# Modulation chunks behind the first attention, expert loads from the state stage on, and expert weights in pieces of 8 KB

## The reference

```python
c_act = silu(c)
mod = c_act @ w_mod + b_mod                 # 6 x 1024 columns
sh1, sc1, gt1, sh2, sc2, gt2 = split(mod, 6)
h = layer_norm(x) * (1 + sc1) + sh1
y = hybrid_mixer(h, ...)                    # state-space mixer + attention, gated, then @ w_o
x = layer_norm(ALPHA * x + (1 + gt1) * y, ln1_g, ln1_b)
h = layer_norm(x) * (1 + sc2) + sh2
gates = top 2 of 16 experts per token       # softmax over 4 groups, 4 experts in each
out = sum_e gates[:, e] * ((silu(h @ w_gate[e]) * (h @ w_up[e])) @ w_down[e])
x = layer_norm(ALPHA * x + (1 + gt2) * out, ln2_g, ln2_b)
```

## Time and profile before

| | us |
|---|---|
| median of three runs | 1687.82 |
| span of the profiled execution | 1684.1 |
| first attention to the loop over experts | 200 to 355 |
| loop over the eight pairs of experts | 355.5 to 585.8 |
| second block | from 600 |
| TensorE busy | 1594.6 (95%) |
| VectorE busy | 936.2 (56%) |
| ScalarE busy | 655.0 (39%) |
| DMA, queue q1 (all loads of SP) | 326.94 MB, 54.2% of 16 engines |

### The profile page before, as it was taken

The page is one execution under the profiler, slowest core; times in us unless marked ns, Lnnn a source line. Parts: engine busy times, 40 slices in busy tenths (PEclk is TensorE's granted clock), DMA queues, the critical chain, the costliest instruction groups (busy, mean ns, idle before and its releaser), DMA issues.

```text
span 1684.1 us, 22446 instructions
## 1 busy us (share of the span) xinstructions
PE 1594.6 (95%) x9391; PEld 1239.9 (74%) x9391; DVE 936.2 (56%) x1380; ACT 655.0 (39%) x962; POOL 27.4 (2%) x89
## 2 busy tenths in 40 slices
PE   5999999989999879999999999999999999999998
PEld 1998655454445468687888899988768778889986
DVE  3876666632222266466675566545456567556653
ACT  2543420111111144565644534435355644544441
POOL 1000010100000000000000000000000000000000
PEclk9999999999999989999999999999999999999999
DMA  9555518999999924423354356545424235536651
GB/s 310 193 177 200 202 55 296 332 383 404 393 357 410 389 97 150 125 70 131 127 197 154 122 179 200 193 152 199 144 85 150 101 125 176 174 120 194 200 176 74
DMA packets 165376, 333.29 MB, mean 198 GB/s; under 512 B 17699, under 2 KB 69157, under 8 KB 165285
## 3 DMA queue, kind: packets, MB, share of 16 engines
q1 hardware_dynamic: 159728, 326.94, 54.2%
q10 hardware_dynamic: 5558, 5.06, 0.9%
HBM read 330.94 MB, written 1.05 MB: 197 GB/s over the span
## 4 chain that ended last, share of the span: by engine, by line
PE 77%; DVE 10%; DMA 7%; ACT 4%; issue 1%; POOL 0%; ACTq 0%; SPq 0%; POOLq 0%; DVEq 0%
PE ps_g L726 19%; PE ps_g L707 15%; PE ps_g L1262 5%; PE ps_g L1130 5%; DMA arena<-in_w_up_dram 4%; PE ps_s L1518 4%; PE ps_p L1518 3%; PE ps_o L774 3%; PE ps_g L867 3%; DVE ring_r L2266 2%; PE ps_p L707 2%; DMA ring<-in_w_mod_dram 1%; PE ps_x L680 1%; PE ps_g L1485 1%; PE ps_g L1406 1%
## 5 line engine op out<-in xcount | busy, mean ns | idle before, releaser
L2266 DVE TENSOR_TENSOR ring_r<-ring,late_w 128x4096 fp32r<-128x4096 f32 (+1 forms) x50 | 217.0, 4339 | 153.4 <-ACT late_w L1834 153.4
L1834 ACT ACTIVATE late_w<-ring 128x4096 fp32r<-128x4096 f32 (+1 forms) x50 | 178.1, 3563 | 126.8 <-PE ps_p L1518 42.8
L726 PE MATMUL ps_g<-hf_high,ring_r 128*128 128x256 f32 x640 | 178.9, 280 | 0.0
L726 PE MATMUL ps_g<-hf_high,late_w 128*128 128x256 f32 x576 | 162.1, 282 | 0.0
L726 PE MATMUL ps_g<-h_t_r,late_w 128*128 128x256 f32 x576 | 161.3, 280 | 0.0
L726 PEld LDWEIGHTS ps_g<-hf_high,ring_r 128*128 128x128 f32 x640 | 121.9, 190 | 0.0
L726 PEld LDWEIGHTS ps_g<-h_t_r,late_w 128*128 128x128 f32 x576 | 108.7, 189 | 0.0
L726 PEld LDWEIGHTS ps_g<-hf_high,late_w 128*128 128x128 f32 x576 | 108.1, 188 | 0.0
L1858 ACT ACTIVATE arena<-arena,neg_max 128x256 f32<-128x256 f32 (+1 forms) x160 | 71.5, 449 | 40.4 <-DVE neg_max L2321 40.4
L1130 PE MATMUL ps_g<-arena 128*64 128x512 f32 x288 | 85.9, 599 | 0.0
L707 PE MATMUL ps_g<-early_w,first_low 128*128 128x512 f32 (+1 forms) x176 | 68.7, 390 | 4.1 <-ACT arena L1820 2.2
(11 more groups left out here) (697 smaller groups left out, 3710.7 us busy)
## 6 DMA issues: line engine op xcount, KB each, us to landing
ring<-in_w_in_dram SPq DMA_DIRECT2D x31, 2048.0 KB, 7.9
ring<-in_w_gate_up_dram SPq DMA_DIRECT2D x44, 1024.0 KB, 7.4
arena<-in_w_down_dram SPq DMA_DIRECT2D x16, 2048.0 KB, 14.3
ring<-in_w_mod_dram SPq DMA_DIRECT2D x10, 2048.0 KB, 11.3
ring<-in_w_down_dram SPq DMA_DIRECT2D x10, 2048.0 KB, 7.9
arena<-in_w_up_dram SPq DMA_DIRECT2D x8, 2048.0 KB, 18.7
ring<-in_w_gate_dram SPq DMA_DIRECT2D x8, 2048.0 KB, 16.0
ring<-in_w_up_dram SPq DMA_DIRECT2D x4, 2048.0 KB, 19.1
```

The costliest lines, as they stand in the source:

```text
L726: ins = pe.matmul(b.ap[:, (f % 2) * SEQ:(f % 2 + 1) * SEQ], a[:, k, f * P:(f + 1) * P], x[:, k, :], start=k == 0 and i == 0, stop=k == nk ...
L1834: act.activation(high_of(name, rnd)[:, 0:n], ring[:, slot, 0:n], ACT.Copy).then_inc(high_ready.sem, 1)
L2266: dve.tensor_tensor(ring_r[:, slot, 0:n], ring[:, slot, 0:n], high_of(name, rnd)[:, 0:n].bitcast(F32), ALU.subtract).then_inc(low_ready.se ...
```

## The change

Chunks 10 and 11 of the modulation are loaded behind `att`, and VectorE adds them up ahead of its gating of the two halves of the attention product. Chunks 6 and 7 are loaded next, and TensorE takes their strips in the state stage, one behind the second `xs` transpose and the other in the middle of the `seg` products; `gs1`, `mod4` and `mod5` follow. The slots of the ring are now in a table. `down1` and `down0` of pair 0 and both gates of pair 1 are loaded during the state stage and the `so` products, `gate1`, `up1`, `up0` and `gate0` of pair 0 as slots come free. The gates of pair 1 have other places in the arena, and small tiles of the loop have moved for that. All expert chunks are cut in pieces of 8 KB: four rows of 512 or two rows of 1024 a piece. So the channels of `h2` stand in groups of four and not of two (`GROUPED`), which the copies of chunks 6 to 9, the norm `normed`, the router's weights and the hidden values of an expert follow.

```diff
-MOD_SUMMED = [8, 9, 4, 10, 11]
+MOD_SUMMED = [8, 9, 10, 11, 4]

 MOD_LATE = (10, 11)
 FIRST_CHUNKS = (MOD_FIRST + ["xbc0"] + [f"xbc{i}" for i in range(1, 4)] + ["q", "k", "v", "z0", "z1", "ga0", "ga1", "mod8", "gs0", "mod9", "att",
-                "gs1", "mod4", "mod5", "so0", "so1", "o0", "o1", "mod6", "mod7"])
+                "mod10", "mod11", "mod6", "mod7", "gs1", "mod4", "mod5", "so0", "so1", "o0", "o1"])
+
+FIRST_SLOTS = [j % 3 for j in range(FIRST_CHUNKS.index("mod6"))] + [1, 2, 0, 1, 2, 0, 1, 2, 0]
+assert len(FIRST_SLOTS) == len(FIRST_CHUNKS)
+LAYER_FIRST_SLOT = 1
...
-        odd_w = arena[:, 0:SLOT].rearrange("p (k n) -> p k n", n=HALF), [arena[:, lo:lo + SLOT // 2].rearrange("p (k n) -> p k n", n=HALF) for lo in (12 * D, GATES_AT - 2 * D)]
-        odd_up = x_rows, arena[:, 14 * D:16 * D].rearrange("p (t n) -> p t n", n=D)
+        odd_w = [arena[:, lo:lo + SLOT].rearrange("p (k n) -> p k n", n=HALF) for lo in (8 * D, 12 * D)]
+        odd_up = x_rows, arena[:, GATES_AT - 2 * D:GATES_AT].rearrange("p (t n) -> p t n", n=D)
...
+        def strips_bank(i):
+
+            return PT if i in (6, 7) else mod_bank(i)
+
+        def by_group(v):
+            return v.rearrange("p (k s q) -> p k q s", s=GROUPED, q=P)
+
+        def in_groups(v):
+            return v.rearrange("p (k q s) -> p k q s", s=GROUPED, q=P)
...
                 ins.then_inc(b.full, 1)
+                if r == 1:
+                    mod_strips(6)
             claim(S, "cb")
             for c in range(TB):
                 for g in range(SSD_GROUPS):
@@ -974,6 +990,8 @@
                                     conv[:, 12 + g, c * P:(c + 1) * P], start=True, stop=True)
             ins.then_inc(S.full, 1)
             for c in range(TB):
+                if c == 1:
+                    mod_strips(7)
                 for g in range(SSD_GROUPS):
...
             product_block("o1", 1, mg_turned)
-            mod_strips(6)
-            mod_strips(7)
             strips_sum(6)
...
-                w = w.rearrange("(k p) n -> p k n", p=P) if name.startswith("down") else w.rearrange("(k p s) n -> p k (s n)", p=P, s=2)
+                w = w.rearrange("(k p s) n -> p k (s n)", p=P, s=2 if name.startswith("down") else GROUPED)
                 sync.dma_start(keys(pair_w[j], w.shape[1], w.shape[2]), w).then_inc(expert_landed[j], 16)
+
+            def load_odd_gate(p, e):
+
+                w = t["w_gate"][0, 2 * p + e].rearrange("(k p s) n -> p k (s n)", p=P, s=GROUPED)
+                sync.dma_start(odd_w[e].rearrange("p (k s) n -> p k (s n)", s=GROUPED), w).then_inc(odd_landed[e], 16)
...
+                if name == "mod5":
+                    sync.wait_ge(G1.full, G1.nth("first", "att1"))
+                    load_expert("down1", 0)
                 if name == "o0":
                     sync.wait_ge(S.full, S.nth("first", "yo"))
                     sync.wait_ge(decay_ready, TB * SSD_GROUPS)
-                    for j, i in enumerate(MOD_LATE):
-                        sync.dma_start(keys(pair_w[4 + j], KD, HALF), sources("first", MOD_CHUNKS[i], 0)[0]).then_inc(late_landed[j], 16)
-                if name == "mod6":
+                    load_expert("down0", 0)
+                    sync.wait_ge(PT.full, PT.nth("first", "yd1"))
+                    load_odd_gate(1, 1)
+                    sync.wait_ge(O.full, O.nth("first", "gy11"))
+                    load_odd_gate(1, 0)
+            for name in ("gate1", "up1", "up0", "gate0"):
+                if name == "up1":
                     sync.wait_ge(O.full, O.nth("first", "mg11"))
                     load_expert("up1", 0)
-                if name in ("mod6", "mod7"):
-                    j = ("mod6", "mod7").index(name)
-                    sync.wait_ge(mod_parts, MOD_SUMMED.index(MOD_LATE[j]) + 1)
-                    load_expert(f"down{j}", 0)
-            for j, name in enumerate(PAIR_CHUNKS[:SLOTS]):
-                part, use, rnd = last[j]
+                    continue
+                part, use, rnd = last[PAIR_CHUNKS.index(name)]
                 where, what = used[part, use]
                 if isinstance(where, Bank):
...
-                w = [t["w_gate"][0, 2 * p + e].rearrange("(k p s) n -> p k (s n)", p=P, s=2) for e in range(2)]
-                sync.dma_start(odd_w[0].rearrange("p (k s) n -> p k (s n)", s=2), w[0]).then_inc(odd_landed[0], 16)
-                for half, dst in enumerate(odd_w[1]):
-                    sync.dma_start(dst.rearrange("p (k s) n -> p k (s n)", s=2), w[1][:, 2 * half:2 * half + 2, :]).then_inc(odd_landed[1], 16)
+                for e in range(2):
+                    load_odd_gate(p, e)
...
-                w = t["w_up"][0, 2 * p].rearrange("(k p s) n -> p k (s n)", p=P, s=2)
+                w = t["w_up"][0, 2 * p].rearrange("(k p s) n -> p k (s n)", p=P, s=GROUPED)
                 for half, dst in enumerate(odd_up):
-                    sync.dma_start(dst[:, :, :], w[:, 2 * half:2 * half + 2, :]).then_inc(odd_up_landed, 16)
+                    sync.dma_start(dst[:, :, :].rearrange("p t n -> p (t n)"), w[:, half, :]).then_inc(odd_up_landed, 16)
...
-            load_gates(1, 1, (rows.sem, rows.at("first", "h2_1")))
             load_up(1, (X.full, X.nth("first", "places")))
...
             act.activation(b_rows[:, :, :], O.ap[:, :].rearrange("p (g n) -> p g n", n=SSD_N), ACT.Copy).then_inc(O.free, 1)
+            keep_strips(6)
             for i in range(TB * SSD_GROUPS):
+                if i == SSD_GROUPS:
+                    keep_strips(7)
                 act.wait_ge(seg_cut, i + 1)
                 act.activation(decay[:, i], decay[:, i], ACT.Exp).then_inc(seg_exp, 1)
...
-            for i in (6, 7):
-                keep_strips(i)
             for i in (6, 7):
                 b = mod_bank(i)
                 act.wait_ge(b.full, b.nth("first", MOD_CHUNKS[i]))
-                act.activation(by_pair(mod_cols(i)), in_pairs(b.ap[:, :]), ACT.Copy).then_inc(b.free, 1)
...
-                if i in MOD_LATE:
-                    place, arrived, count = pair_w[4 + i - 10], late_landed[i - 10], 16
-                else:
-                    slot, count, _ = PLACE["first", MOD_CHUNKS[i]]
-                    place, arrived = ring[:, slot, :], landed[slot]
-                w, total = keys(place, KD, HALF), mod_cols(i)
-                dve.wait_ge(arrived, count)
+                slot, count, _ = PLACE["first", MOD_CHUNKS[i]]
+                w, total = keys(ring[:, slot, :], KD, HALF), mod_cols(i)
+                dve.wait_ge(landed[slot], count)
...
             for half in range(2):
+                add_modulation(MOD_LATE[half])
                 for tb, b in enumerate(G):
...
-                    add_modulation(MOD_LATE[tb], range(i * KD // 2, (i + 1) * KD // 2))
...
-                for s in range(2):
-                    st.done(dve.scalar_tensor_tensor(paired(h_rows[:, tb, :], s), x_rows[:, tb, :].rearrange("p (k q s) -> p s k q", s=2, q=P)[:, s],
+                for s in range(GROUPED):
+                    st.done(dve.scalar_tensor_tensor(paired(h_rows[:, tb, :], s), x_rows[:, tb, :].rearrange("p (k q s) -> p s k q", s=GROUPED, q=P)[:, s],
                                                      mean_var[:, tb, 0:1], paired(mod[:, 4, :], s), ALU.subtract, ALU.mult))
...
-                dve.tensor_tensor(expert_t[:, 0, :], expert_t[:, 1, :], M1.ap[:, :], ALU.mult).then_inc(M1.free, 1)
+                dve.tensor_tensor(by_pair(expert_t[:, 0, :]), in_pairs(expert_t[:, 1, :]), in_pairs(M1.ap[:, :]), ALU.mult).then_inc(M1.free, 1)
```

65 lines of the change are left out of this document (33 added, 32 removed).

## The result

The changed kernel takes 1692.51 us (median of 20 runs, 1684.3 to 1698.84), the kernel before 1687.54 beside it (20 runs, 1683.66 to 1689.69). The ratio is 1.0026, its 95% interval 1.0017 to 1.0036 (the ratios are formed from the runs beside each other and differ a little from the quotient of the two medians, here 1.0029): slower, where 1686.7 and "no change" were forecast. 1692.51 lies within the range of 1680.5 to 1694 and just under the 0.3% that the prediction had set for a change, but the sign is not in doubt. The profiled execution took 1690.55 us, with a span of 1688.8 (before: 1684.1). The two traces are compared from front to back.

The account below looks back on a forecast made before the run. The prediction took a chain 77% TensorE as the bound, with transfers counting only where it runs through them. State stage +4.2, its end −1.0, loop −4.3 made −1.1 us: 1686.7 us, 8 in 10 for 1680.5 to 1694.

Parts of the forecast that it names:

- State stage: Up to gs1: VectorE's sums of chunks 10 and 11 and TensorE's strips of 6 and 7 cost +4.2 us.
- End of the stage: After the o products: no wait for ScalarE's copy of chunk 7, but four passes for two; −1.0 us.
- what the end of the stage gives back: Step pricing the strips' removal behind the o products by VectorE's waits: −1.0 us, bounds −1.3 and +0.1.
- 8 KB pieces: Expert loop: 0.153 us less per chunk over 28 chunks shortens the waits for up1, −4.3 us, bounds 0 and −7.9.
- The clock loss of 1.9: Loop, product after the third up1 wait, slowed by a lower clock: assumed to stay; −1.9 us more if it goes.
- The rivals on the rate: Loop transfers with 8 KB pieces: all waits go (21%), piece size hardly matters (16%), or the rate falls (13%).
- that first rival: Loop: larger pieces end all waits, needing 431 and 436 GB/s; −6.6 us in all, so 1681.2 us; chance 21%.
- Earlier loads: Loop: loading the first expert pairs sooner gains 0, since the queue was already empty when pair 2's loads went out.
- the bound of 2.7: Loop: most that earlier loads could gain, the 2.7 us by which sixteen chunks came later than the formula.
- The counting of chunks: Loop: up1 waits end sixteen and twelve chunks after loads issued at 362.63 and 498.37, at time per chunk plus 2.9 us.
- Other edits at nothing: Paired up-gate multiply, regrouped copies and changed arena places cost 0; the multiply's extra time falls in VectorE's 1.74 us idle.
- "slower" rival: Loop's 28 chunks: larger pieces lower the rate to 396 GB/s, +8.3 us in all, so 1696.1 us; chance 13%.

Follow-up runs that it names:

- e1: Kernel before with nothing but the 8 KB pieces and the layouts to match, old load order kept: 1685.24 us, ratio 0.9981.
- e10: Kernel before with 8 KB pieces and h2's first product in two passes over half rows instead of four strided ones: 1682.30 us, ratio 0.9969.
- e2: Changed kernel with its chunk order and early loads, but 4 KB pieces and layouts as before: 1694.20 us, ratio 1.0036.
- e12: Changed kernel's order with 16 KB pieces and five idle matmuls ahead of h2's transposes: 1687.61 us, ratio 0.9997.
- e11: Kernel before with 16 KB pieces and one idle matmul ahead of the first h2 transpose: 1682.24 us, ratio 0.9964.
- e9: Changed kernel itself, run and profiled a second time: 1691.38 us, ratio 1.0019.
- e5: Changed kernel with five idle matmuls on TensorE in its idle time ahead of the first h2 transpose: 1687.76 us, ratio 0.9996.
- e7: Changed kernel, sums of chunks 10 and 11 cut to two passes, strips of 6 and 7 to one matmul each: 26.2 us from first transpose to loop.
- e6: Changed kernel with VectorE's sums of chunks 10 and 11 cut from eight passes to two each: 20.5 us from first h2 transpose to loop.
- e13: Kernel before with 8 KB pieces, h2 in two passes, and four idle VectorE copies ahead of the shift: 1692.90 us, ratio 1.0038.
- e8: Kernel before with 16 KB pieces, but for one gate and one up of odd pairs in 8 KB halves: 1683.70 us, ratio 0.9973.
- e4: Kernel before with chunks 6 and 7 summed by one matmul each instead of eight: 1937 us, with tokens sent to other experts.

## Why the prediction was wrong

*State stage, forecast +4.2, found +6.0 (by the means; +6.9 in the first pair of profiles).* The mechanism was right and a size was off. In the pair of profiles the three parts are: first `xs` transposes 4.1 later (219.98 to 224.08; forecast +1.5), segment products 4.6 later, so 0.5 for the strips of chunk 6 (+0.8; the 224.6 and 225.4 in that sum are times of the fourth `xs` transposes, 223.22 before, not of the third), then 1.9 for those of chunk 7 (+1.9) and 0.4 in a longer wait ahead of them. The mis-sized term is the first. I had chunk 10 issued at 196.07 and landed 8.0 later, as a lone load had the earlier trace rows. It was issued at 196.98 and took 9.8, so its sum and two gatings ended at 215.2 and not at 212.7, and as no idle time of VectorE was left behind that, all of it was passed on. The 8.0 was of another matrix, `w_att_o`. Chunk 10 takes 9.0 to 9.8 us in the eight profiles of the new order, with nothing ahead of it in the queue, while the chunk of `w_in` in its place takes 7.6 to 8.0 in the nine of the old one. The trace of before had a closer row: a lone chunk of `w_mod`, issued at 174.61, landed 9.2 later. Why `w_mod` lands later no run shows.

*End of the stage, forecast −1.0, found −0.3.* ScalarE's wait went as said. The four passes were priced at +0.3 from their element count; they took +0.96, within the bound of +1.4.

*What is late next.* This is the step that failed: "what the end of the stage gives back" asked only what VectorE waits for. It never asked what TensorE does in the time that its strips leave. They had filled 323.4 to 327.9, and TensorE went from one piece of work to the next with 0.7 us between. Without them it has nothing to do for 5 us, and its clock was 0.50 behind it in both profiles of the changed kernel, at a price of 3.8 and 5.9 us there. Filling the gap, with nothing else changed, moved the new order from 1.0019 (or 1.0026) to 0.9996, and the old order with a gap from 1.0038 to 1.0004, though there the profiles don't show where. The Trainium skill ("TensorE: Matmul & The Clock Gate", section "Why this matters for your kernels") warns of idle gaps between bursts of matmuls. These runs agree: behind all six gaps of 3.66 to 5.02 us in this place the first instruction ran at half clock. The forecast had weighed none of it, though the trace of before had it in plain sight, behind the loop, in TensorE's timeline:

```profile
594.14 1.12 PE L1194 MATMUL ps_x<-ident,x_rows 128*128 128x128 f32 x4 [4.80 <-DVE x_rows L2929]
```

Four transposes that take 0.66 at full clock take 1.12 behind 4.80 us of idle time, and each of the other 16 traces shows the same there.

*8 KB pieces, forecast −4.3.* Right, and the best part of it. Summed lateness of `up1` fell from 7.9 to 3.7 in e1 (−4.2) and 2.9 in the changed kernel (−5.0). The rate was forecast at 423 GB/s from the step between 2 and 4 KB; long stretches show 422 to 423 (e1, e10). The clock loss of 1.9, left in, was gone in the first profile, which is why the loop shrank by 6.8 there; e1 still lost clock (0.96 in 420:450). The rivals on the rate fall: it neither stayed, nor fell, nor came near the 431 and 436 of the first. One argument against that first rival had been misread: "no stretch of several us here has more than 410" does not agree with the earlier trace rows, where five slices in a row, about 335 to 342 us, stand at 417 to 420.

*Earlier loads, forecast 0.* Nearly right: 1.1 less waiting in e2, inside the bound of 2.7, and no difference between e12 and e11. The counting of chunks carries: in the changed kernel the loads that had gone out at 362.63 and 498.37 go out at 373.01 and 505.47, and at 423 GB/s twelve chunks and 2.9 make 62.4 us, against 568.51 − 505.47 = 63.0; sixteen make 82.2, against 457.11 − 373.01 = 84.1.

*Other edits at nothing.* Right. VectorE's multiply takes 1.09 instead of 0.69 and VectorE still idles 1.33 ahead of its next step, which is within what was said to be covered.

*The sum.* Forecast −1.1. The same terms as found are +6.0 − 0.3 − 5.5 (the loop to its last scatter in the eight profiles with 8 KB pieces, 228.3 on the mean, against 233.8) = +0.2, and the missing one, +3.8 to +5.9, gives about what the medians say (+5.0, and +3.1 in e9). With the gap filled, e5 stands at 0.9996, close to the forecast's 0.9993, but that is partly luck: the state stage and its end cost 2.5 us more than forecast, the loop gave back 1.2 more. My "slower" rival had put its price on the loop's rate and so had the wrong place.

Not settled: why the clock stays down for 3 us behind one gap and for more than 10 behind another. Six profiles have a long gap ahead of the `h2` transposes. Behind 5.02 us the changed kernel twice and e7 had the long fall (route products 6.85 to 6.86, 24.5, 26.6 and 26.2 us to the loop), and e6 the short one (3.90, and 20.5 us); e2 and e13, behind 4.06 and 3.66, had the short one too (3.98 and 3.90, both 20.5 us). So the length of the gap does not decide it, and by the profiles the price in one execution lies between nothing and 5.9 us (against the 20.7 of before). The 4 to 5 us by which e5 is faster are what it comes to over a dozen runs.

## What to carry to other kernels

When work leaves an engine's queue, ask what the engine does in its place: TensorE standing idle for 5 us between two bursts cost as much as the 3.8 us of work that was moved, or more, in both profiles of the changed kernel (3.8 and 5.9), nothing in one of e6, and five useless matmuls won 0.2 to 0.3% back. Look for such a gap in the trace at hand first: here one stood behind the loop. An idle stretch on another engine covers moved work only as far as its inputs are there in time; count from the landing of a load of the same matrix, not of another one (9.2 against 8.0 here). And take a change with two ideas apart: the pieces alone are 0.2 to 0.3% faster than before, the order alone 0.36% slower.

## What the runs showed of the hardware

- The rate by piece size, all engines busy: 410 GB/s at 4 KB, 423 at 8 KB, 428 with most pieces at 16 KB (505 to 560 us of e2, e1 and e8). With 16 engines that is 159.8, 309.9 and 612.5 ns a piece, so a doubling saves 9.7 and then 7.3 ns: close to the 9.5 ns that the prediction read from the slower of two 2 KB stretches.
- TensorE's clock was at half already in the first instruction after idle times of 3.66, 4.06 and 5.02 us ahead of the `h2` transposes and of 4.80 behind the loop (four transposes in 1.1 us each time, 23 times in 17 traces), and at full after 0.65 to 1.38 us. It falls in this stretch in the kernels without a long gap too, somewhat later (0.83 in 340:350 of e1, 0.66 of e8); from the first transpose to the loop those take 19.2 to 22.3 us, those with a gap 20.5 to 26.6.
- A load of 2 MB in pieces of 2 KB with nothing ahead of it in the queue landed after 7.6 to 8.0 us when cut from `w_in` or `w_att_o`, and after 8.8 to 9.8 when cut from `w_mod` (chunk 10, and the one issued at 174.61 before); the cause is open.
- Chunk 7 in the old order kept TensorE waiting 0.67 us before and 1.21 to 2.04 in the kernels with larger pieces (1.68 in e1). That the larger pieces ahead of it in the queue are the cause is not shown: it landed 9.4 us after its issue before, 9.9 to 10.7 with larger pieces, but 10.1 in e4 too, where the pieces are of 4 KB.
- VectorE's passes with a longer stride cost more than their elements: four of 256 took 2.37 us where two of 512 took 1.41, two over half rows each with the same result 2.11.
